# Reordering the joins of a four-mixer network: where VectorE issues the norm, the residual update and the split remainders

## The reference

```python
def rmsnorm(x, g):
    y = x * lax.rsqrt(jnp.mean(jnp.square(x), axis=-1, keepdims=True) + 1e-6)
    return y * g
def modulate(h, shift, scale):
    return h * (1.0 + scale) + shift
...
for i in range(4):
    hl = modulate(rmsnorm(xl, mix_pre_g[i]), mod_l[0], mod_l[1])
    yl = mixer[i](hl)                                   # context tokens too, in layers 0 and 1
    xl = xl + mod_l[2] * rmsnorm(yl, mix_post_g[i])
    hl = modulate(rmsnorm(xl, ffn_pre_g[i]), mod_l[3], mod_l[4])
    xl = xl + mod_l[5] * rmsnorm(swiglu(hl, ffn_w13[i], ffn_w2[i]), ffn_post_g[i])
```

## The kernel before

| join | tokens | next | split | modulation matmuls |
|---|---|---|---|---|
| J1 before layer 0 | 512 | MLA | yes | no |
| J2 middle of layer 0 | 512 | FFN | yes | yes |
| J3 into layer 1 | 512 | Hyena | yes | yes |
| J4 middle of layer 1 | 512 | FFN | yes | yes |
| J5 into layer 2 | 512 | S5 | no | no |
| J6 middle of layer 2 | 256 | FFN | yes | no |
| J7 into layer 3 | 256 | Fourier | no | no |
| J8 middle of layer 3 | 256 | FFN | yes | no |

## Time and profile before

### The profile page before, as it was taken

The page is one execution under the profiler, slowest core; times in us unless marked ns, Lnnn a source line. Parts: engine busy times, 40 slices in busy tenths (PEclk is TensorE's granted clock), DMA queues, the critical chain, the costliest instruction groups (busy, mean ns, idle before and its releaser), DMA issues.

```text
span 2296.0 us, 31537 instructions
## 1 busy us (share of the span) xinstructions
PE 2113.6 (92%) x13233; PEld 1653.2 (72%) x13233; DVE 1145.5 (50%) x1941; ACT 865.1 (38%) x1416; POOL 120.5 (5%) x185
## 2 busy tenths in 40 slices
PE   4999889999999999988999999997739899998998
PEld 2755557677777767754557778885737799977997
DVE  2322543645556566636154554665391545536454
ACT  2442224533333353220243333335532544525444
POOL 0000000102001100010010210020000000000000
PEclk8999979999999999999999999999569899999999
DMA  6334341535434546442145553344532455324553
GB/s 250 129 135 168 110 147 38 173 131 172 177 132 166 190 168 221 150 152 74 37 152 185 199 203 118 115 156 156 218 147 92 137 186 184 119 85 152 183 182 109
DMA packets 228683, 344.23 MB, mean 150 GB/s; under 512 B 9238, under 2 KB 192321, under 8 KB 226300
## 3 DMA queue, kind: packets, MB, share of 16 engines
q1 hardware_dynamic: 218016, 313.41, 39.6%
q0 software_dynamic: 9808, 28.53, 4.1%
q10 hardware_dynamic: 716, 0.26, 0.0%
HBM read 319.76 MB, written 26.61 MB: 151 GB/s over the span
## 4 chain that ended last, share of the span: by engine, by line
PE 85%; DVE 9%; DMA 3%; ACT 2%; issue 1%; SPq 1%; ACTq 0%; DVEq 0%
PE bank L953 21%; PE bank L954 20%; PE bank L955 20%; PE bank L397 4%; PE bank L819 4%; PE bank L864 2%; PE bank L1705 1%; PE bank L1341 1%; PE bank L2405 1%; DMA mod_ring<-mod_w 1%; PE bank L637 1%; DMA arena<-mod_w 1%; PE bank L2038 1%; PE bank L627 1%; PE bank L1317 1%; PE bank L1659 1%
## 5 line engine op out<-in xcount | busy, mean ns | idle before, releaser
L953 PE MATMUL bank<-h_hi,w_hi 128*128 128x512 f32 (+1 forms) x1480 | 512.5, 346 | 11.5 <-DVE h_lo L725 11.0
L954 PE MATMUL bank<-h_lo,w_hi 128*128 128x512 f32 (+1 forms) x1480 | 504.7, 341 | 0.0
L955 PE MATMUL bank<-h_hi,w_lo 128*128 128x512 f32 (+1 forms) x1480 | 504.5, 341 | 0.0
L915 DVE TENSOR_TENSOR w_lo<-ring,w_hi 128x1024 fp32r<-128x1024 f32 (+1 forms) x282 | 323.9, 1186 | 312.8 <-ACT w_hi L910 312.7
L953 PEld LDWEIGHTS bank<-h_hi,w_hi 128*128 128x128 f32 x1480 | 283.2, 191 | 51.4 <-DVE h_lo L725 13.9
L910 ACT ACTIVATE w_hi<-ring 128x1024 fp32r<-128x1024 f32 (+1 forms) x282 | 274.0, 1019 | 102.7 <-PE bank L955 100.8
L955 PEld LDWEIGHTS bank<-h_hi,w_lo 128*128 128x128 f32 x1480 | 283.0, 191 | 32.2 <-issue 0.2
L954 PEld LDWEIGHTS bank<-h_lo,w_hi 128*128 128x128 f32 x1480 | 283.6, 192 | 29.1 <-issue 0.2
L953 PE MATMUL bank<-g_hi,w_hi 128*128 128x512 f32 (+1 forms) x704 | 241.3, 343 | 0.0
L954 PE MATMUL bank<-g_lo,w_hi 128*128 128x512 f32 (+1 forms) x704 | 237.0, 337 | 0.0
L955 PE MATMUL bank<-g_hi,w_lo 128*128 128x512 f32 (+1 forms) x704 | 236.7, 336 | 0.0
(11 more groups left out here) (322 smaller groups left out, 2932.4 us busy)
## 6 DMA issues: line engine op xcount, KB each, us to landing
ring<-ffn_w SPq DMA_DIRECT2D x120, 1024.0 KB, 5.1
mod_ring<-mod_w SPq DMA_DIRECT2D x88, 1024.0 KB, 7.1
ring<-ffn_w SPq DMA_DIRECT2D x16, 768.0 KB, 4.5
ring<-hy_w_in SPq DMA_DIRECT2D x12, 1024.0 KB, 5.3
arena<-mod_w SPq DMA_DIRECT2D x8, 1024.0 KB, 17.5
s_in_weights<-arena POOLq DMA_DIRECT2D x32, 256.0 KB, 3.1
s_out_weights<-arena POOLq DMA_DIRECT2D x16, 512.0 KB, 4.4
ring<-s_w_glu SPq DMA_DIRECT2D x8, 1024.0 KB, 5.7
```

Source lines behind the costliest of these rows:

```text
L915: nc.vector.tensor_tensor(self.lo[:, i % SPLIT, a:b], self.w.slot(i)[:, a:b], self.hi[:, i % SPLIT, a:b].bitcast(F32), ALU.subtract).then_ ...
L953: nc.tensor.matmul(o, w[0], v[0], start=first, stop=False)
L954: nc.tensor.matmul(o, w[0], v[1], start=False, stop=False)
L955: return nc.tensor.matmul(o, w[1], v[0], start=False, stop=last)
```

## The change

Three things are moved, and nothing is added or taken away in the work itself.

1. On DVE, `remain(0, 0)` goes from ahead of `scaled(0)` to behind `normed(0)`. The two second halves, `remain(0, 1)` and `remain(1, 1)`, stood behind `remainder(2)` and `remainder(3)`, and now both stand behind `remainder(2)`.
2. On DVE, `update(1)` goes ahead of `normed(0)`, and in the loop `normed(k)` is now issued just ahead of the `scaled(k+1)`, `update(k+1)` and `remainder(k)` of its own turn, no longer one block ahead.
3. On ACT, `round(1, 1)` goes from ahead of block 0 to behind the rounding of block 1.

```diff
@@ Join.scalar
                     self.first.round(act, 1, 0)
-                    if self.parts:
-                        self.first.round(act, 1, 1)
...
                         nc.scalar.activation(h_hi[:, k, 0:self.n], SQ[:, k, 0:self.n], ACT.Copy).then_inc(h_rounded, 1)
+                        if k == 1:
+                            self.first.round(act, 1, 1)
                         if k == 5:
                             self.first.round(act, 2, 0)
@@ Join.vector
+                    dve.wait_ge(*self.spreads.after(1))
+                    scaled(0)
                 else:
                     dve.wait_ge(*self.summed.after(1))
                     nc.vector.tensor_copy(b, bank[5][0:rows, 0:P]).then_inc(j_small, 1)
-                if self.first:
-                    self.first.remain(dve, 0, 0)
-                if self.post:
-                    dve.wait_ge(*self.spreads.after(1))
-                scaled(0)
...
                 nc.vector.reciprocal(rq, rq).then_inc(j_small, 1)
-                update(0)
-                scaled(1)
+                if self.post:
+                    update(0)
+                    scaled(1)
+                    update(1)
                 dve.wait_ge(*self.spreads.after(2 if self.post else 1))
-                normed(0)
-
                 for k in range(KD):
-                    update(k + 1)
-                    scaled(k + 2)
-                    normed(k + 1)
+                    normed(k)
+                    if k == 0 and self.first:
+                        self.first.remain(dve, 0, 0)
+                    if self.post and k:
+                        scaled(k + 1)
+                        update(k + 1)
                     if self.parts:
                         remainder(k)
                         if k == 0:
                             self.first.remain(dve, 1, 0)
-                        if k in (2, 3):
-                            self.first.remain(dve, k - 2, 1)
+                        if k == 2:
+                            self.first.remain(dve, 0, 1)
+                            self.first.remain(dve, 1, 1)
                         if k == KD - 1:
                             self.first.remain(dve, 2, 0)
```

More of the change, by code:

```diff
@@ L708, in scaled @@
                 def scaled(k):
-                    if self.post and k < KD:
+                    if k < KD:
                         nc.vector.tensor_tensor(Y[:, k, 0:n], Y[:, k, 0:n], bank[5][:, 0:n], ALU.mult).then_inc(j_step, 1)
                 def update(k):
-                    if self.post and k < KD:
+                    if k < KD:
                         dve.wait_ge(*self.t.after(k + 1))
@@ L717, in normed @@
                 def normed(k):
-                    if k < KD:
-                        if self.post:
-                            dve.wait_ge(*self.x.after(k + 1))
-                        nc.vector.tensor_tensor(SQ[:, k, 0:n], x[:, k, 0:n], bank[4][:, 0:n], ALU.mult).then_inc(x_normed, 1)
+                    if self.post:
+                        dve.wait_ge(*self.x.after(k + 1))
+                    nc.vector.tensor_tensor(SQ[:, k, 0:n], x[:, k, 0:n], bank[4][:, 0:n], ALU.mult).then_inc(x_normed, 1)
                 def remainder(k):
```

## The result

The kernel after the change takes 2322.49 us (median of 4 runs, 2320.32 to 2325.91), the kernel before 2298.63 us in the runs beside it (4 runs, 2293.76 to 2303.26): a ratio of 1.0105, with a 95% interval of 1.0081 to 1.0131. Timed once more beside other kernels it took 2321.28 us against 2302.50 us of the kernel before, a ratio of 1.0082 (1.0060 to 1.0104). The forecast was 2322.5 us.

A forecast was written before the change was run, and what follows sets the result against it. PE, busy for 92% of the span, was taken to bound the kernel. Join terms 7.1 + 4.9 + 4.1 + 4.0 + 3.6 + 1.0 = 24.7 us on 2297.8 gave 2322.5 us, range 2317 to 2328.

The forecast's parts named there:

- The loop through ACT: In each split-product join, DVE stands for ACT every block: period 3.17 us with 512 tokens, 1.92 with 256.
- J1, J2 and J4: Joins before layer 0, mid layer 0 and mid layer 1, 512 tokens: 7.1, 4.9 and 4.0 us later.
- S(0): Start of `normed(0)` in a join: 0.84 us earlier before layer 0, 0.53 later mid layer 0, 0.93 earlier with 256 tokens.
- J6 and J8: Joins in the middle of layers 2 and 3, 256 tokens, split product: 1.8 us later each, 3.6 together.
- J7: Join into layer 3, 256 tokens, no split product: DVE instructions waiting on their predecessor cost 1.0 us.
- J5: Join into layer 2, 512 tokens, no split product: counted as nothing.
- "it now comes some 0.2 us too late for PE", in J3: Join into layer 1: 3.9 us, plus the weight rounding behind GpSimd's memset reaching PE 0.2 us late, 4.1 us.
- "ACT's moves cost nothing": Moving `round(1,1)` behind block 1 fits ACT's idle time, no cost; without cover, about 1 us a join.
- Rival (a), the clock: PE's clock falls behind the new stands in six lead-ins: up to 8.6 us more, 2331 us; chance 0.13.
- Rival (b): A later PE wait set by something unmoving gives back about half: 2310 to 2315 us; chance 0.10.
- Rivals (c) and (d): Stand on ACT doesn't bite, 2.7 us faster, 2295; or only idle time is reordered, nothing moves; together 0.07.
- "DVE idle 0.65 us in J1 to J4, 0.5 in J6 and J8": Sign in the next profile: DVE idle ahead of each `h_lo`, about 0.65 us a block with 512 tokens, 0.5 with 256.

The follow-up runs named there:

- pieces_only: The kernel before with only the moved `remain` and `round` pieces (parts 1 and 3), DVE's loop as it was: 2302.41 us, ratio 1.0006.

## Why the prediction was right

- **The loop through ACT** was right: DVE stands ahead of each `remainder`, `h_hi` ends it, the order of one instruction decides. The period was foretold as 3.17 and 1.92 and is 3.11 and 1.88. The 2.57 us of latency was read at block 0; from block 1 on it is 2.50. Seven times 0.05 or so is the 0.3 us by which J1, J2 and J4 came out below their terms.
- **S(0)** was right in J1 (5.36 us after the join's first step instead of 6.21, foretold 0.84 earlier) and in J2 to J4 (0.53 later, as foretold).
- **J6 and J8** came out as 1.1 and 1.3 instead of 1.8. In J6 `normed(0)` starts 1.31 us earlier than before, not 0.93: the spread into `bank[5]` and the small steps ahead of the root took less (the spread 0.71 us instead of 1.22). These 0.4 us lie in the trace of before, where `normed(0)` stands 6.56 us behind the join's first step; three other traces with the old start have 6.17. The shorter period is another 0.24.
- **J7** was right, 1.03 us in one trace and 0.7 in the other. It is also where the trace and the rule of the Trainium skill (VectorE: DVE Perf Modes, The DRAIN you can't avoid) part: by that rule J7 would have gained 0.4.
- **J5** was put at nothing, and is -0.2 and +0.5 in two traces: no change that can be told.
- **The step that was mis-sized** is "it now comes some 0.2 us too late for PE", in J3. The 0.2 us is there, but the step followed only GpSimd's clears, ACT and `w_lo`. `h_lo(7)` also starts 2 MB of loads ahead of a modulation panel. The new order makes PE take `h_lo(7)` as soon as it is there; before, it lay ready for 2.9 us. This slack was what hid the transfer. The term is 3.6 + 2.1 = 5.7 instead of 4.1. It and the smaller terms of J1, J2, J4, J6 and J8 (together 2.0 us less) nearly cancel.
- **The hit to 0.1 us is luck.** Beside these two errors that cancel, the forecast started from 2297.8 us, the median of three runs, where the kernel before mostly takes 2302.5, and the second timing of the change gave 18.8 us. The runs bear out the mechanism and a cost of some 20 to 24 us, not 24.7 to the tenth.
- **"ACT's moves cost nothing"** was right within what was measured: `pieces_only` is at 1.0006.
- **Rival (a), the clock**, does occur and costs next to nothing in the lead-ins. In J1, J2 and J4, behind the stands of 2.2 to 2.4 us ahead of block 3, matmuls run for some 3 us at the lower level, 0.63 us instead of 0.40. In J2 and J4 PE then works through blocks 4 to 7 without a stand: the slow matmuls have used up the idle time. The last block still starts within 0.2 us of where `h_lo(7)` would let it. The two traces of the kernel after settle it: behind block 3's stand the clock fell in J2 in the first and not in the second, in J3 in the second and not in the first, and J2 costs 4.6 us and J3 3.6 in both. This is also why PE's waits on `h_lo` rose to 23.7 in one trace and 27.7 in the other and not to the 30 us foretold: in part, PE is slow where it would have stood. What the clock costs in attention and Hyena differs from trace to trace with both orders, and stays open. **Rival (b)** did not occur; what came behind a join was an added wait. **Rivals (c) and (d)** are refuted by `normed` spaced 3.11 us.
- "DVE idle 0.65 us in J1 to J4, 0.5 in J6 and J8" was wrong in size: 0.50 and 0.33. The latency is 0.07 us shorter, and the rows count idle time from the end of `update`, 0.09 us after the point at which DVE can start the next instruction. It is 1.8 in J1, which has no `scaled` and `update` to fill it.

## What to carry to other kernels

Where two engines hand a block to and fro, issue the first engine's next step ahead of the step that waits: otherwise the period is the whole round trip plus its own instruction (here 2.50 + 0.61 = 3.11 us), whatever the busy shares say. When an end of a join moves, look at all that its last semaphore releases, its transfers included, and at how long the released thing lay ready before: slack that has gone can come back on the matmul engine as a wait some 15 us later. When parts of a change are timed apart, a piece that costs 1.1 us in one order can be free in another, so their sum is not the whole.

## What the runs showed of the hardware

- A modulation panel of 1 MB took 9.9 us from issue to landing when issued 8.2 us behind the start of the loads, and 13.4 us when issued 4.5 us behind it: both land 18 us after that start. 1 MB less among them gave 2.9 us, 0.5 MB more cost 1.2 us. The transfer engines were busy for 0.97 of the last 10 us before the landing.
- An ACT scale and shift over 128x512 takes 0.81 us, over two halves 1.09, and a plain rounding of 128x512 takes 0.63.
- The granted clock fell behind a stand of PE of 2.37 us (0.79 over the 8 us around it) and was back at 1.00 in the next 8 us, with PE busy throughout. In a second trace of the same kernel it stayed at 1.00 around a stand of 2.33 us in the same place.
- A DVE instruction that waits for the one right ahead of it starts 0.72 us behind it at 128x512 (433.28 to 434.00 in J2) and 0.45 at 128x256 (J7); without such a wait the distance is 0.60 and 0.33.
